# A ninth slot in the ring of expert weights, with its tables moved and turns of 36 parts

## The chip, the cores and the metric

The kernel runs on one core of one Trainium2 chip. The metric is the device time of one execution in microseconds (us). The core has TensorE (matmul), VectorE, ScalarE, GpSimd and SyncE. SyncE does no arithmetic here; it issues nearly all transfers, in the order in which they stand in its program.

## What is computed

One decoder layer for 256 prompt tokens and 8 sampled sequences of 4 tokens: a combined projection, retention and block-sparse attention, an output projection, and then a layer of 32 experts of which each token takes 4. All in float32. The change touches the expert layer alone:

```python
def moe(h, router_w, router_b, w_gu, b_gu, w_d, b_d):
    tok = h.reshape(-1, D_MODEL)
    logits = tok @ router_w + router_b
    top_v, top_i = lax.top_k(logits, TOP_K)
    top_w = jax.nn.softmax(top_v, axis=-1)
    gates = jnp.einsum('tk,tke->te', top_w, one_hot(top_i, N_EXPERTS))
    def expert(acc, xs):
        wgu, bgu, wd, bd, g = xs
        u = tok @ wgu + bgu
        glu = jnp.minimum(u[:, ::2], 7.0)
        lin = jnp.clip(u[:, 1::2], -7.0, 7.0)
        a = glu * jax.nn.sigmoid(1.702 * glu) * (lin + 1.0)
        return acc + g[:, None] * (a @ wd + bd), None
```

An expert has 8 MB of gate and up weights (1024 x 2048) and 4 MB of down weights (1024 x 1024), 384 MB for the 32.

## The kernel before

All of SBUF is one array, `arena`, of 53176 words on each of 128 partitions, and every tile is a fixed place in it (`at(start, dims)`). The program is written by hand for each engine, with semaphores between them.

**The stages.** Until about 310 us the projections, the two kinds of attention and the output projection run. Then comes the router, up to 325 us: TensorE multiplies by the router weights, VectorE takes the best four experts of each of three token tiles (`picked` marks them), and TensorE counts with three triangular or full matrices of ones (`earlier`, `ones`) which rank a token has at its expert (`count`, line 831). From the ranks VectorE makes selection matrices (`one_hot`, 1672), with which TensorE gathers up to 64 tokens of each expert of a pair (`gather`, 844).

**The expert loop.** 32 experts are 16 pairs. TensorE's `pair` (926) does the gate products of the first expert of a pair (four parts), its down products (two parts), the same for the second, and between them the transposes, the scatter of the pair before (`combine`) and the gather of the pair to come. `last_pair` (977) does pair 15 in another order. Lines 1063 to 1067 run pairs 0 to 13 in a loop of two pairs a pass and pairs 14 and 15 behind it. VectorE and ScalarE have loops of one pair.

**The ring.** An expert's weights come in `PARTS` = 6 parts of 2 MB, four of gate and up weights and two of down weights, 192 in all. Part n goes to slot n % 8. The eight slots of 4096 words lie in the first 32768 words of the arena, in space of the earlier stages, so that each opens when its stage is through (`PLACE`). SyncE issues parts 0 to 7 one by one behind such waits (lines 2019 to 2044); part 0 goes out at 263 us, parts 6 and 7 once the output projection is done, at 310. After that part n+8 waits until TensorE has used part n (`w_used`), in a loop of `TURN` = 24 parts a pass (2046 to 2051) and in straight code for the last 16 parts. The last one is fetched in two halves. TensorE waits for each part on the semaphore of its slot (`wt_in`).

**The tables.** `late` is one transfer of 304 KB (line 2030) with a count `iota`, the two counting matrices and an `expert` matrix of 32 columns. It stands at the end of the region Q (3328 words), which also holds the router's scratch: logits, `hot`, `picked`, `gates` sums and the scratch for pairs that need more rounds. Region MX (2304 words) follows Q. The scratch of further rounds is only used where an expert has more than 64 tokens; in these runs that branch isn't entered.

**Before the first pair.** Behind the gather of pair 0 TensorE counts the tokens of all experts (`count(3, ...)`, 1043), transposes the gates (1048), does two products that only keep it busy (`stay_awake`) and starts pair 0 once ScalarE has copied the gathered tokens and VectorE has made `esel` (1746). On VectorE the totals of the pairs (1734 to 1741), the quarter copies (1790) and the copy of the transposed gates (1794) stand ahead of that `esel`.

Of the kernel before, what the change touches and what calls it, by code (L numbers as in the profile page):

```python
# [23 lines left out]
I32 = mybir.dt.int32  # L24
# [21 lines left out]
RING = 8  # L46
# [122 lines left out]
def build_kernel(nc, t, table, outs):  # L169

    with ExitStack() as ctx:
# [20 lines left out]
        gate_slot = [at(WSLOT * place, 2, F2) for place in PLACE]  # L192
        down_slot = [at(WSLOT * place, 4, D) for place in PLACE]
# [25 lines left out]
        gain_in = at(cur, P); cur += P  # L219
        stat = at(cur, 64); cur += 64  # L220
        own_s = at(cur, 2, NS); cur += 2 * NS
# [39 lines left out]
        assert cur <= WORDS, cur  # L261

# [25 lines left out]
        sel = at(MX, TILES, 2, SLOTS)  # L288
        selg = at(MX + 384, TILES, 2, SLOTS)
        sgt = at(MX + 768, TILES * P)  # L290
        esel = at(MX + 1152, 2, SLOTS)
        rankm = at(MX + 1280, TILES, E + 2)
        gates = at(MX + 1280 + TILES * (E + 2), TILES, E + 2)
# [15 lines left out]
        pair_n = at(Q + 1032, PAIRS)  # L309
        flag = at(Q + 1048, 4, PAIRS)  # L310
        n_over_f = at(Q + 1112, 1)
        n_over_i = at(Q + 1113, 1).bitcast(I32)
        before = at(Q + 1114, 2, 64)
        work = at(Q + 1242, EXTRA, 64)
        work_f = at(Q + 2394, 2, EXTRA)
        work_i = at(Q + 2430, 2, EXTRA).bitcast(I32)
        pair_of = at(Q + 2466, 64)
        round_of = at(Q + 2530, 64)
        picked_off = at(Q + 2594, TILES, E)
        late = at(Q + 3328 - late_cols, late_cols)  # L320
        assert Q + 3328 - late_cols >= Q + 2690

        def late_const(name):
            a, n = table[name]
            return late[:, a - ncols:a - ncols + n]

        iota, earlier, ones = late_const("iota"), late_const("earlier"), late_const("ones")
# [88 lines left out]
        def _(pe):  # L416
# [409 lines left out]
            pe.wait_ge(late_in, 16)  # L826
# [14 lines left out]
            count(2, ones, 1, start=False, stop=True).then_inc(rank_full, 1)  # L841

# [1115 lines left out]
        def _(sp):  # L1958
# [51 lines left out]
            def load_turn(t):  # L2010
                load_part(t // PARTS, t % PARTS, t % RING)
# [99 lines left out]
```

## Time and profile before

| | |
|---|---|
| median of 3 runs | 1268.71 us (1266.96 to 1270.87) |
| the profiled execution | 1270.82 us |
| its span, first to last instruction | 1269.0 us |
| TensorE busy (matmuls) | 1207.8 us, 95% |
| VectorE, ScalarE, GpSimd busy | 384.2, 232.7, 120.3 us |
| moved | 500.64 MB, mean 395 GB/s |
| mean granted TensorE clock | 0.983 |

The span is cut on the page into 40 slices of 31.7 us:

```profile
PE   6999998699999999999999999999999999999997
PEclk8999999889899999999999999999999999999999
DMA  8999889968799999999999999999999999999994
GB/s 334 378 363 357 314 297 326 387 243 319 280 415 430 428 429 429 428 429 429 429 427 429 429 428 429 429 429 427 429 429 428 430 428 429 428 428 428 427 428 199
```

Each digit is the busy share of a slice in tenths, the last row what was moved. Both TensorE and the 16 DMA engines look full from the twelfth slice on. Matmuls are pipelined and their ends are modelled, so a busy TensorE isn't proof that it works at its peak, and which of the two bounds the loop has to be read from the chain of work that ended last and from the times between issue and landing of the transfers.

### The profile page before, as it was taken

Reading aid. Unit: us, or ns where it says so; the run is one execution under the profiler, and the core shown is the slowest. Engines: PE = TensorE matmul, PEld = TensorE weight load, DVE = VectorE, ACT = ScalarE, POOL = GpSimd, SP = SyncE. Lnnn points to the kernel's source line nnn. Section 1 sums busy time; section 2 is a strip of 40 time slices with the busy share of each in tenths; the row PEclk is TensorE's granted clock in tenths of the full one; section 3 lists DMA queues with packets and bytes.
Section 4 is the critical chain, followed back from the end, with each engine's and each line's share of the span. In section 5 each row is a group of like instructions: output and inputs, shape, how many; then the busy total and the mean of one; then the engine's idle time right before and its main releaser. Section 6 shows DMA issues by size and latency. Waiting matters only on the chain.

```text
span 1269.0 us, 17410 instructions
## 1 busy us (share of the span) xinstructions
PE 1207.8 (95%) x7256; PEld 517.4 (41%) x7256; DVE 384.2 (30%) x552; ACT 232.7 (18%) x529; POOL 120.3 (9%) x117
## 2 busy tenths in 40 slices
PE   6999998699999999999999999999999999999997
PEld 3455445345534434343433434343434434343432
DVE  4999964153411211111122111111112211111113
ACT  3021153024201121110112112010102121111103
POOL 2222446641000000000000000000000000000000
PEclk8999999889899999999999999999999999999999
DMA  8999889968799999999999999999999999999994
GB/s 334 378 363 357 314 297 326 387 243 319 280 415 430 428 429 429 428 429 429 429 427 429 429 428 429 429 429 427 429 429 428 430 428 429 428 428 428 427 428 199
DMA packets 56604, 500.64 MB, mean 395 GB/s; under 512 B 6393, under 2 KB 6801, under 8 KB 27761
## 3 DMA queue, kind: packets, MB, share of 16 engines
q1 hardware_dynamic: 42128, 430.55, 81.1%
q0 software_dynamic: 14432, 69.47, 14.7%
q8 instruction: 32, 0.52, 0.2%
q14 instruction: 12, 0.09, 0.0%
HBM read 495.29 MB, written 4.72 MB: 394 GB/s over the span
## 4 chain that ended last, share of the span: by engine, by line
PE 61%; DMA 26%; DVE 7%; issue 4%; ACT 1%; SPq 0%; POOL 0%; DVEq 0%; POOLq 0%; ACTq 0%
PE psum L940 22%; DMA arena<-w_gate_up 21%; PE psum L971 12%; PE psum L852 6%; DVE arena L1430 5%; DMA arena<-w_down 3%; PE psum L858 2%; PE psum L502 2%; PE psum L697 2%; PE psum L870 2%; PE psum L589 2%; PE psum L882 2%; DMA arena<-cache_k,arena 1%; PE psum L889 1%; PE psum L428 1%
## 5 line engine op out<-in xcount | busy, mean ns | idle before, releaser
L940 PE MATMUL psum<-arena 128*64 128x512 f32 x1920 | 422.7, 594 | 15.7 <-DMA arena<-w_gate_up 15.6
L940 PEld LDWEIGHTS psum<-arena 128*64 128x64 f32 x1920 | 134.8, 137 | 300.1 <-issue 265.0
L1758 DVE TENSOR_SCALAR arena<-psum 128x512 f32<-128x512 f32 x32 | 22.1, 692 | 682.8 <-PE psum L940 643.5
L971 PE MATMUL psum<-arena 128*64 128x512 f32 x960 | 212.6, 595 | 0.0
L1096 ACT ACTIVATE arena<-psum 64x512 f32<-64x512 f32 (+3 forms) x184 | 93.5, 509 | 370.2 <-PE psum L971 170.7
L1430 DVE STREAM_TRANSPOSE arena<-arena 128x2048 f32<-128x2048 f32 x32 | 121.4, 3920 | 3.1 <-PE psum L488 1.9
L971 PEld LDWEIGHTS psum<-arena 128*64 128x64 f32 x960 | 66.4, 137 | 124.2 <-issue 122.4
L502 PE MATMUL psum<-arena 128*128 128x512 f32 x224 | 107.1, 617 | 0.5 <-ACT arena L1096 0.4
L1313 ACT ACTIVATE arena<-arena 128x512 f32<-128x512 f32 x30 | 18.9, 631 | 419.4 <-DVE arena L1758 419.4
L1096 ACT ACTIVATE arena<-psum,arena 128x128 f32<-128x128 f32 (+2 forms) x182 | 53.6, 397 | 171.2 <-PE psum L502 115.8
L852 PE MATMUL psum<-arena 128*128 128x128 f32 x512 | 80.1, 302 | 0.4 <-DVE arena L1679 0.4
L852 PEld LDWEIGHTS psum<-arena 128*128 128x128 f32 x512 | 69.3, 206 | 17.7 <-issue 14.0
L1904 POOL DMA_INDIRECT arena<-cache_v,arena x64 | 70.4, 1100 | 50.9 <-PE psum L589 24.2
L870 PE MATMUL psum<-arena 128*128 128x512 f32 x128 | 63.5, 617 | 0.0
L502 PEld LDWEIGHTS psum<-arena 128*128 128x128 f32 x224 | 40.3, 192 | 46.6 <-issue 46.6
L1781 DVE TENSOR_TENSOR arena<-psum,arena 128x512 f32<-128x512 f32 (+1 forms) x80 | 48.0, 633 | 12.6 <-PE psum L870 12.6
L589 PE MATMUL psum<-arena 128*32 128x512 f32 x256 | 33.1, 653 | 13.5 <-DMA arena<-cache_v,arena 9.0
L488 PE MATMUL psum<-arena 128*32 128x128 f32 x1024 | 35.4, 280 | 7.6 <-DVE arena L1451 4.7
L1890 POOL DMA_INDIRECT arena<-cache_k,arena x32 | 32.3, 1010 | 100.3 <-DVE arena L1430 91.0
L488 PEld LDWEIGHTS psum<-arena 128*32 128x32 f32 x1024 | 26.7, 111 | 32.4 <-DVE arena L1430 17.0
L882 PE MATMUL psum<-arena 32*64 32x512 f32 x248 | 33.7, 613 | 1.0 <-DVE arena L1746 1.0
L870 PEld LDWEIGHTS psum<-arena 128*128 128x128 f32 x128 | 21.6, 188 | 28.8 <-issue 23.6
(242 smaller groups left out, 724.3 us busy)
## 6 DMA issues: line engine op xcount, KB each, us to landing
arena<-w_gate_up SPq DMA_DIRECT2D x128, 2048.0 KB, 29.7
arena<-w_down SPq DMA_DIRECT2D x63, 2048.0 KB, 32.9
arena<-w_in SPq DMA_DIRECT2D x7, 2048.0 KB, 18.3
arena<-w_out SPq DMA_DIRECT2D x2, 2048.0 KB, 13.9
out<-arena SPq DMA_DIRECT2D x4, 512.0 KB, 3.0
out<-arena POOLq DMA_DIRECT2D x1, 2048.0 KB, 12.5
arena<-w_down SPq DMA_DIRECT2D x2, 1024.0 KB, 34.0
arena<-x_prompt SPq DMA_DIRECT2D x2, 512.0 KB, 5.6
```

What stands on the lines that cost most here:

```text
L488: last = mm(psum[NS * c:NS * (c + 1), bank, P * (n % 4):P * (n % 4 + 1)], qk[:, g, 4 * c + x, :], kt[:, 4 * c + x, :], start=x == 0, stop= ...
L502: last = mm(psum[:, bank, :], h_t[:, k, tile * P:(tile + 1) * P], w[:, k, :], start=k == 0, stop=k == KC - 1)
L589: last = mm(psum[NS * s:NS * (s + 1), 6 + g, :], pt_sb[:, v % 2, j * P + s:(j + 1) * P:4], v_raw(n)[:, s, 512 * r:512 * (r + 1)], start=False,
L852: mm(o, hn[:, tile, cols], sel[:, tile].rearrange("p a b -> p (a b)"), start=tile == 0, stop=False, skip_group_check=True)
L870: last = mm(psum[:, 3 + half, :], sgt[:, P * tile:P * (tile + 1)], out2[:, 512 * half:512 * (half + 1)], start=True, stop=True)
L882: mm(psum[64 * g:64 * (g + 1), b, :], esel[E * b:E * (b + 1), e, :], bgu[E * b:E * (b + 1), g, :], start=True, stop=False, skip_group_chec ...
L940: last = mm(psum[64 * g:64 * (g + 1), b, :], xt[:, 2 * kk + m, lhs], gate_slot[slot][:, m, c:c + 512], start=False, stop=kk == 3 and m == ...
L971: last = mm(psum[64 * g:64 * (g + 1), 2, :], at_sb[:, m, SLOTS * q:SLOTS * (q + 1)], down_slot[slot][:, m, 512 * g:512 * (g + 1)], start=q ...
L1096: return nc.scalar.activation(out, in_, ACT.Copy, scale=scale)
L1430: v.transpose(kt_sb[:, u % 2, :].rearrange("p (e b r) -> p r e b", e=16, b=32), k_raw[:, u % 4, :]).then_inc(k_trans, 1)
L1781: v.tensor_tensor(dst, got, dst, ALU.add).then_inc(comb_added, 1)
L1904: pool.indirect_dma_start(out=v_raw(n)[:, s, :], out_offset=None, in_=cv, in_offset=bass.IndirectOffsetOnAxis(ap=row, axis=0), bounds_chec ...
```

## The change

- `RING` is 9. The ninth slot is words Q to Q + 4095: all of region Q and the first 768 words of MX. The order of the parts stays; part n goes to slot n % 9.
- What lived there moves: the tables `iota` and `earlier` to words of the softmax scratch of the attention (`LT`), `ones` to the place of `gain_in`, the selection matrices, `rankm` and `gates` 768 words up in MX, the scratch of further rounds to the cosine table's place behind the router weights and to other dead places.
- The tables come in three transfers in place of one. They are issued before `x_sample` and wait for the second normalisation of the attention (`o_norm` 2), where before they were issued behind part 2.
- Part 8 is issued behind part 7, after waits for both counts of the router (`rank_full` 2) and for `gates_ready`.
- The count over all experts moves from behind the gather to ahead of it, and to PSUM bank 0.
- TensorE's loop has three pairs a pass and five passes, with pair 15 behind it; SyncE's has 36 parts a pass and four passes, with 39 parts of straight code behind it.

```diff
-RING = 8
+RING = 9
...
-        gate_slot = [at(WSLOT * place, 2, F2) for place in PLACE]
-        down_slot = [at(WSLOT * place, 4, D) for place in PLACE]
...
+        SLOT_AT = [WSLOT * place for place in PLACE] + [Q]
+        assert len(SLOT_AT) == RING and MX == Q + 3328
+        gate_slot = [at(a, 2, F2) for a in SLOT_AT]
+        down_slot = [at(a, 4, D) for a in SLOT_AT]
...
-        late = at(Q + 3328 - late_cols, late_cols)
...
+        late_at = {"iota": LT, "earlier": LT + 320, "expert": LT + 448}
...
             count(2, ones, 1, start=False, stop=True).then_inc(rank_full, 1)
+            for tile in range(TILES):
+                last = mm(psum[:, 0, 0:E], ones, picked[:, tile, :], start=tile == 0, stop=tile == TILES - 1)
+            last.then_inc(rank_full, 1)
...
             gather(0, 1)
-            for tile in range(TILES):
-                last = count(3, ones, tile, start=tile == 0, stop=tile == TILES - 1)
-            last.then_inc(rank_full, 1)
             pe.wait_ge(gates_ready, 1)
...
-                return lambda part: ((12 * half + part) % RING, i * 48 + 16 * ((12 * half + part) // RING + 1))
+                return lambda part: ((12 * half + part) % RING, i * 64 + 16 * ((12 * half + part) // RING + 1))
...
-            with pe.Fori(0, PAIRS // 2 - 1) as i:
-                pair(i * 2, in_turn(i, 0), True)
-                pair(i * 2 + 1, in_turn(i, 1), True)
-            pair(PAIRS - 2, in_turn(PAIRS // 2 - 1, 0), True)
-            last_pair(PAIRS - 1, in_turn(PAIRS // 2 - 1, 1))
+            with pe.Fori(0, PAIRS // 3) as i:
+                for third in range(3):
+                    pair(i * 3 + third, in_turn(i, third), True)
+            last_pair(PAIRS - 1, in_turn(PAIRS // 3, 0))
...
             sp.wait_ge(*mark["pt7"])
+            sp.wait_ge(o_norm, 2)
+            a = table["iota"][0]
+            sp.dma_start(at(LT, 448), t["shape_consts"][:, a:a + 448]).then_inc(late_in, 16)
+            for dst, name in ((ones, "ones"), (late_const("expert"), "expert")):
+                a, n = table[name]
+                sp.dma_start(dst, t["shape_consts"][:, a:a + n]).then_inc(late_in, 16)
             sp.wait_ge(y_zero, 1)
...
-            sp.dma_start(late, t["shape_consts"][:, ncols:ncols + late_cols]).then_inc(late_in, 16)
...
             load_turn(7)
-
-            TURN = 24
-            with sp.Fori(0, (E * PARTS - RING) // TURN) as i:
+            sp.wait_ge(rank_full, 2)
+            sp.wait_ge(gates_ready, 1)
+            load_turn(8)
+
+            TURN, TURNS = 36, 4
+            with sp.Fori(0, TURNS) as i:
                 for u in range(TURN):
                     part = RING + u
                     sp.wait_ge(w_used, i * TURN + (u + 1))
-                    load_part(i * 4 + part // PARTS, part % PARTS, part % RING)
-            for part in range(RING + (E * PARTS - RING) // TURN * TURN, E * PARTS):
+                    load_part(i * 6 + part // PARTS, part % PARTS, part % RING)
+            for part in range(RING + TURNS * TURN, E * PARTS):
```

## Rows read from the trace of the kernel before

**Rows 1.** The chain that ended last, from 341 us: start, duration, what.

```profile
341.52 13.88 PE psum L940 x64
...
397.53 13.88 PE psum L940 x64
...
740.74 30.58 DMA arena<-w_gate_up
...
1065.01 3.65 PE psum L940 x16
...
1123.74 3.65 PE psum L940 x16
...
1183.62 3.65 PE psum L940 x16
...
1202.16 7.04 PE psum L991 x32
...
1242.36 3.65 PE psum L1007 x16
```

**Rows 2.** Windows: length, busy us (records) by engine, clock, DMA share, GB/s.

```profile
400.00:500.00 100.00, 100.00 (x505) 39.95 (x502) 19.41 (x33) 12.91 (x25) 0.00 (x0) 1.00 1.01 428
...
335.00:340.00 5.00, 4.45 (x24) 2.88 (x22) 2.33 (x10) 3.32 (x9) 0.00 (x0) 0.91 0.89 374
340.00:345.00 5.00, 4.57 (x26) 1.48 (x28) 1.68 (x5) 0.14 (x1) 0.00 (x0) 1.00 0.04 18
345.00:350.00 5.00, 5.00 (x26) 1.66 (x24) 0.00 (x0) 0.00 (x0) 0.00 (x0) 1.00 0.77 252
```

**Rows 3.** Transfers of line 2008 in 800 to 1200 us.

```profile
DMA to landing us min/median/max: 29.7/33.0/36.4
```

**Rows 4.** Timeline of VectorE and ScalarE before pair 0: start, duration, instruction.

```profile
327.92 0.26 DVE L1732 TENSOR_TENSOR arena<-arena 128x96 f32<-128x96 f32 x1
...
339.51 0.55 DVE L1794 COPY arena<-psum 32x384 f32<-32x384 f32 x1
...
336.66 2.17 ACT L1096 ACTIVATE arena<-psum,arena 128x128 f32<-128x128 f32 x8 [12.26 <-PE psum L858]
```

**Rows 5.** Timeline of TensorE around the gather, and one gather in the loop.

```profile
324.60 1.10 PE L443 MATMUL psum<-arena 128*128 128x512 f32 x2
326.11 2.05 PE L852 MATMUL psum<-arena 128*128 128x128 f32 x8 [0.40 <-DVE arena L1679]
...
336.55 0.85 PE L831 MATMUL psum<-arena 128*128 128x32 f32 x6
...
340.43 1.09 PE L882 MATMUL psum<-arena 32*64 32x512 f32 x8 [0.98 <-DVE arena L1746]
...
382.57 1.23 PE L852 MATMUL psum<-arena 128*128 128x128 f32 x8
```

**Rows 6.** Windows of one microsecond where the clock changes.

```profile
325.00:326.00 1.00, 0.71 (x2) 0.00 (x0) 0.93 (x4) 0.00 (x0) 0.00 (x0) 0.81 1.05 442
...
335.00:336.00 1.00, 1.00 (x7) 0.99 (x5) 0.00 (x0) 0.00 (x0) 0.00 (x0) 0.57 1.18 492
```

**Rows 7.** Timeline of SyncE's issues, and the second normalisation on VectorE.

```profile
225.10 2.35 SPq L2015 DMA_DIRECT2D arena<-router_b  x1
...
291.29 0.33 SPq L2023 DMA_DIRECT2D arena<-x_sample  x1
...
295.82 1.38 SPq L2030 DMA_DIRECT2D arena<-shape_consts  x1
...
287.47 0.75 DVE L1482 TENSOR_SCALAR arena<-psum,arena 128x512 f32<-128x512 f32 x1
```

**Rows 8.** Packets, MB and share by queue, in 340:450, 450:1100 and 1100:1215 us.

```profile
q8 instruction: 4, 0.07, 0.2%
...
q1 hardware_dynamic: 19128, 278.54, 100.7%
...
q8 instruction: 3, 0.05, 0.2%
```

More of the change, by code:

```diff
@@ L218, in build_kernel @@
         gain = at(cur, 28); cur += 28
-        gain_in = at(cur, P); cur += P
+        gain_in = at(cur, P)
+        ones = at(cur, P); cur += P
         stat = at(cur, 64); cur += 64
+        LT = cur
         own_s = at(cur, 2, NS); cur += 2 * NS
@@ L287, in build_kernel @@
         at_last = at(HT, 4, P)
[L288 to L293, printed above, removed]
+        sel = at(MX + 768, TILES, 2, SLOTS)
+        selg = at(MX + 1152, TILES, 2, SLOTS)
+        sgt = at(MX + 1536, TILES * P)
+        esel = at(MX + 1920, 2, SLOTS)
+        rankm = at(MX + 2048, TILES, E + 2)
+        gates = at(MX + 2048 + TILES * (E + 2), TILES, E + 2)
+        assert 2048 + 2 * TILES * (E + 2) <= 2304
         squares = at(HT, D)
@@ L308, in build_kernel @@
         picked = at(Q + 936, TILES, E)
[L309 to L318, printed above, removed]
+        RW = C0 + table["cos"][0]
+        pair_n = at(RW, PAIRS)
+        flag = at(RW + 16, 4, PAIRS)
+        n_over_f = at(RW + 80, 1)
+        n_over_i = at(RW + 81, 1).bitcast(I32)
+        work_f = at(RW + 82, 2, EXTRA)
+        work_i = at(RW + 118, 2, EXTRA).bitcast(I32)
+        before = at(RW + 154, 2, 64)
+        assert 282 <= (KC + 1) * E
+        pair_of = at(Z + 4352, 64)
+        round_of = at(Z + 4416, 64)
+        work = at(HT, EXTRA, 64)
         picked_off = at(Q + 2594, TILES, E)
-        late = at(Q + 3328 - late_cols, late_cols)
-        assert Q + 3328 - late_cols >= Q + 2690
+        late_at = {"iota": LT, "earlier": LT + 320, "expert": LT + 448}
+        assert LT + 480 <= HT and table["earlier"][0] == table["iota"][0] + 320
         def late_const(name):
-            a, n = table[name]
-            return late[:, a - ncols:a - ncols + n]
-        iota, earlier, ones = late_const("iota"), late_const("earlier"), late_const("ones")
+            return at(late_at[name], table[name][1])
+        iota, earlier = late_const("iota"), late_const("earlier")
         rw = at(C0 + table["cos"][0], KC, E)
@@ L825, in _ @@
             logits(1).then_inc(lg_full, 1)
-            pe.wait_ge(late_in, 16)
+            pe.wait_ge(late_in, 48)
             def count(tile, lhs, src, **flags):
@@ L1054, in in_turn @@
             def in_turn(i, half):
-                return lambda part: ((12 * half + part) % RING, i * 48 + 16 * ((12 * half + part) // RING + 1))
+                return lambda part: ((12 * half + part) % RING, i * 64 + 16 * ((12 * half + part) // RING + 1))
             def in_extra(n):
-                return lambda part: (part % RING, n * 32 + (16 * (part // RING) - 112)) if part % RING < 4 else \
-                    (part, n * 16 + 144)
-            with pe.Fori(0, PAIRS // 2 - 1) as i:
-                pair(i * 2, in_turn(i, 0), True)
-                pair(i * 2 + 1, in_turn(i, 1), True)
-            pair(PAIRS - 2, in_turn(PAIRS // 2 - 1, 0), True)
-            last_pair(PAIRS - 1, in_turn(PAIRS // 2 - 1, 1))
+                return lambda part: (part % RING, n * 32 + (16 * (part // RING) - 144)) if part % RING < 3 else \
+                    (part, n * 16 + 96)
+            with pe.Fori(0, PAIRS // 3) as i:
+                for third in range(3):
+                    pair(i * 3 + third, in_turn(i, third), True)
+            last_pair(PAIRS - 1, in_turn(PAIRS // 3, 0))
             more = extra_pairs(pe)
@@ L1688, in _ @@
             dve.wait_ge(router_in, 32)
-            dve.wait_ge(late_in, 16)
+            dve.wait_ge(late_in, 48)
             for tile in (0, 2, 1):
```

6 lines of the change are left out of this document (3 added, 3 removed).

## The prediction

> **What bounds the kernel now.** I read the chain that ended last first, because two engines look full on the page. In it [rows 1] TensorE sets the pace at first: the first gate product of pair 0 starts at 341.52 us, that of pair 1 at 397.53, so a pair takes 56.01. At 740.74 a transfer of expert weights enters the chain, and from there the same point of each pair comes every 58.73 us (1065.01 to 1123.74). Twelve parts of 2 MB in 58.73 us are 4.89 us a part, 429 GB/s, and the windows show that rate from 400 us on already [rows 2]. So the transfers never rest in the expert loop, also while TensorE seems to lead: they are the bound, and TensorE only works off the lead of eight parts that it starts with, 58.73 - 56.01 = 2.72 us a pair. Issue to landing says the same: 33 us, nearly seven parts in flight [rows 3].
>
> A stream that never rests is only shortened by an earlier start or fewer bytes. The windows show where it rested [rows 2]: 374 GB/s in 335 to 340, 18 in 340 to 345, 252 in 345 to 350. Against 429 that loses 5 x (0.13 + 0.96 + 0.41) = 7.5 us. There all eight slots are full and TensorE has not yet emptied the first (a part takes it 13.88 / 4 = 3.5 us from 341.5 on). The slack of TensorE against the stream: at 56.01 a pair, pair 15 would start at 341.52 + 15 x 56.01 = 1181.7; it starts at 1202.16 [rows 1]. That is 20.5 us.
>
> **Part by part.**
> *Ninth slot.* Part 8 is issued once gates are ready, at 328.2 [rows 4], behind parts 6 and 7, which keep the queue busy until about 340 [rows 2]. It so fills 4.89 of the 7.5 us of rest; the 11 us between issue and need are its cover. From then on part n+9 waits for the use of part n, as part n+8 did: the stream keeps the same rhythm against TensorE with one part less to go, **-4.89**. What is queued behind the new waits on SyncE is only the loop, which waits for TensorE's first part anyway.
>
> *All pairs counted ahead of the gather.* Six records (0.85 us, 336.55) move to before the stay-awake product at 324.60 [rows 5]. That product then ends at about 326.5 to 327.2 instead of 325.7, and the gather, which began at 326.11, starts 0.4 to 1.1 us later. The clock fell to the 1.2 GHz level at 325.6 (mean 0.81 in that microsecond) and was back at 2.4 late in the microsecond from 335 (0.57) [rows 6]; work pushed past the rise runs twice as fast, so the gather ends only 0.2 to 0.6 later. ScalarE took 2.17 us from 336.66 to copy it, to 338.83 [rows 4]; that becomes 339.0 to 339.4. VectorE's side was later: its totals, flags, quarter copies and the copy of 339.51 (0.55) led to TensorE's start at 340.43, with 0.98 idle [rows 4, 5]. The totals and copies now run during the gather, where VectorE was idle for 9 us, and the transposes that feed the copy follow the gather at once. Late next are ScalarE's copy and the second stay-awake product (twice the 1.10 us of the one at 324.60 less its overlap, from about 337.4), both near 339.4. TensorE starts 0.9 us earlier (bounds 0 and 1.2), hence also the restart of the stream: **-0.9**. It leaves 7.5 - 4.9 - 0.9 = 1.7 us of rest.
>
> *Tables moved.* Instead of one issue of 1.38 us at 295.82, SyncE makes three once the second normalisation is through (287.47 + 0.75), ahead of the issue at 291.29 [rows 7]. Three such are 4.1 us, ending at 292.4: x_sample and parts 1 and 2 go out about 1.2 us later, from part 3 on SyncE is level again, and 304 KB leave the busy queue. The slowest issue of 128 short rows near by took 2.35 us [rows 7]; three of them make part 1 4 us and part 3 some 2.6 us later. The first case costs nothing and the last 1 us, beyond the 1.7 us of rest. I take **0**.
>
> *Loop bodies of three pairs.* TensorE's loop grows from two pairs to three, SyncE's from 24 parts to 36. Fetches of instructions show as queue 8. In 340 to 450, the first pass, it moved 4 packets of 16 KB; from 450 to 1100 none; after the loop it moves again [rows 8]. So two pairs stay resident. 505 + 502 records in 100 us [rows 2] are 564 in a pair's 56; the 1,108 records of 110 us took 4 packets, 277 a packet. The body held was thus four packets and its ends, six or seven. Three pairs are 1,692 records: 6.1 packets, eight with the ends, nine with the one fetched ahead. No row shows nine held. If they are not, each of the four returns fetches up to nine again, 36 packets. Their price: three packets in 115 us at 0.2% of 16 engines are 1.2 us of one engine each [rows 8]. The first one after the loop made a pair 59.88 us, 1.15 more; the next twelve parts took 58.74 again (1183.62 to 1242.36) though further packets fell there [rows 1, 8], so they go to different engines. 36 x 1.15 to 1.5 / 16 = 2.6 to 3.4; I take **+3.0**. The ends are 0 (held) and 36 x 1.15 / 3 = 13.8 (each three cost as the three after the loop did). I choose the refetch because the new body is half as long again as the longest that a row shows held. The tail and the moved scratch words change no count of instructions: 0.
>
> The Trainium skill, page "Runtime: NRT & Kernel Launch", section "Instruction fetch mechanics", speaks against this change: TensorE's instruction memory is a FIFO of 128 KiB, 2048 instructions, in blocks of 16 KiB, and a taken branch to a block outside the window forces a fetch. By that rule nine blocks don't fit into eight and the time is 1265.9; were the body held, 1262.9. The trace agrees on the 16 KB and shows at least six blocks held; its sentence on a window of two pages is not borne out.
>
> **Sum.** -4.89 - 0.9 + 0 + 3.0 = -2.8. The profiled execution had a span of 1269.0 and a time of 1270.8: 1266.2 and 1268.0. Against the median of the runs, 1268.7, it is **1265.9**.
>
> **Rivals.**
> 1. *The longer body is held*, or only the block at its seam is fetched again (2 packets a return, 8 in all, 0.6 us). For it: nothing shows a limit. Then -5.8 or -5.2: 1262.9 to 1263.5.
> 2. *The gap is smaller than in this profile.* With the gather at 2.4 GHz (8 records in 1.23 us, not 2.05 [rows 5]) TensorE starts up to 4.4 us earlier, the stream rests less, and part 8 ends after TensorE's first part. The runs spread over 4 us, and the profiled one is among the slowest, which speaks for it. The gain then falls by up to 2 us, the same as with the late issues above; with refetches 1267 to 1268.
> 3. *Slower: each return of TensorE's loop stands still until the block has come.* Four stalls of X delay pair 15 to 1181.7 - 0.9 + 4X; the slack of 20.5 us hides them until X = 5.3. With X = 8 TensorE becomes the bound and pair 15 starts at 1212.8, 10.6 us late: 1279.3. Slower by over 0.3% from X = 6.3. For it: transfers wait 33 us in the loaded queues [rows 3]; against it: packets of queue 8 hold an engine only 1.2 us, and no stall shows in the first pass. Fetches at 13.8 us would give 1276.7, on the same side.
> 4. *Nothing gained though part 8 is early*, if the start of TensorE slips (1.2 GHz in the first two parts: the first takes 3.5 us longer, the second outlasts a transfer by 2.1): 1269.4 to 1271.5.
>
> **Chances.** Forecast 0.45 (own range 1264.5 to 1267.5), rival 1 0.27, rival 2 0.13, rival 3 0.10, rival 4 0.05. A measurement tells about 0.3%, 3.8 us, from no change: faster means under 1264.9. Rival 1 and a fifth of the forecast and little else lie there, together 0.38; 0.52 within; 0.10 slower. The range runs from 1261.5 (rival 1 with the whole rest of 7.5 us gone) to 1270, leaving out rival 3 and part of 4.
>
> **What would show it.** The windows at 340 to 350 near 429 GB/s but for 1.7 us; a SyncE issue near 328; landing in the settled loop at 38 us rather than 33; TensorE's first gate product at 340.6; starvation of TensorE beginning some two pairs later (5 us at 2.72 a pair). The queue-8 row decides between forecast and rival 1: near 68 packets or 32; the settled pair 58.7 to 59. Wrong would be the forecast if the stream's rate fell for another reason, or if TensorE's pairs showed gaps at every third.

## The result and the profile after

| | before | changed |
|---|---|---|
| median, min to max (5 runs each) | 1266.96 us (1265.82 to 1270.87) | 1259.31 us (1258.33 to 1260.89) |
| ratio, 95% interval | | 0.9934 [0.9915, 0.9952] |
| profiled execution, its span | 1270.82, 1269.0 us | 1259.37, 1257.6 us |
| mean granted clock of it | 0.983 | 0.986 |

The changed kernel is 7.65 us faster in these runs by the medians. The forecast was 1265.9, in a range of 1261.5 to 1270, so the time lies below the range. The same kernel was timed twice more, in two jobs of the experiments (e_after_again and e_after_third), on chips where all kernels take about 30 us longer ahead of the router: 4.9 and 6.6 us by the medians, with ratios of 0.9971 [0.9956, 0.9987] and 0.9955 [0.9939, 0.9971]. The comparisons are of fast runs; the one slow run, 4778.74 us in e_warm_before, is left out.

First the row on which forecast and first rival part. This is the page's list of queues for the changed kernel, and under it the queue's rows for the windows 340 to 450, 450 to 1100 and 1100 to 1215 us (queue: packets, MB, share), as in [rows 8].

```profile
q8 instruction: 32, 0.52, 0.2%
...
q8 instruction: 4, 0.07, 0.2%
...
q8 instruction: 2, 0.03, 0.0%
...
q8 instruction: 1, 0.02, 0.1%
```

32 packets, as many as in before, not 68. The two between 450 and 1100 are at 454.7 and 481.3 us, still in the first pass, which ends at 505; at the four returns of the loop nothing is fetched. The body of three pairs is held.

The windows around the start of pair 0 (columns as in [rows 2]):

```profile
330.00:335.00 5.00, 5.00 (x36) 3.79 (x35) 0.31 (x1) 1.15 (x5) 0.00 (x0) 1.00 1.02 429
335.00:340.00 5.00, 4.79 (x25) 1.40 (x25) 1.87 (x5) 2.31 (x5) 0.00 (x0) 1.00 0.98 415
340.00:345.00 5.00, 5.00 (x26) 1.62 (x24) 0.00 (x0) 0.00 (x0) 0.00 (x0) 1.00 0.96 364
345.00:350.00 5.00, 5.00 (x26) 1.68 (x24) 0.00 (x0) 0.00 (x0) 0.00 (x0) 1.00 1.00 426
400.00:500.00 100.00, 100.00 (x510) 40.72 (x508) 19.96 (x34) 15.11 (x33) 0.00 (x0) 1.00 1.01 427
```

Against 429 GB/s the three from 335 to 350 lose 5 x (0.03 + 0.15 + 0.01) = 1.0 us, where [rows 2] lost 7.5. The stream hardly rests any more. SyncE's timeline shows why (start, duration, line, how many):

```profile
309.18 32.23 SPq L2012 DMA_DIRECT2D arena<-w_gate_up  x4
```

The group of four is parts 6 to 9. Its third, part 8, is out at 327.8 (the end of the group when the timeline is cut at 330 us); its last, part 9, goes out at 341, once TensorE has used part 0.

TensorE ahead of pair 0 (timeline), which answers to [rows 5]:

```profile
323.79 1.47 PE L848 MATMUL psum<-arena 128*128 128x32 f32 x6
325.07 2.05 PE L448 MATMUL psum<-arena 128*128 128x512 f32 x2
326.92 1.67 PE L860 MATMUL psum<-arena 128*128 128x128 f32 x8
...
334.07 1.88 PE L448 MATMUL psum<-arena 128*128 128x512 f32 x4
336.16 1.09 PE L890 MATMUL psum<-arena 32*64 32x512 f32 x8 [0.21 <-ACT arena L1100]
337.18 4.08 PE L948 MATMUL psum<-arena 128*64 128x512 f32 x18
```

The six counting records are now ahead of the gather (323.79). What comes last before pair 0 (its bias products, here line 890) is ScalarE's copy, with 0.21 us of idle time, where VectorE's `esel` cost 0.98. The first gate product is at 337.2 instead of 341.5, 4.3 us earlier. Only 0.7 of that is the change's (measured in e_count_ahead below); 2.5 is the clock, which in the profile of before was low for 10.2 us in the gather [rows 6] and here for 6.9 (321.3 to 328.2, from the granted clock of one-microsecond windows), and 1.1 comes from the stages ahead of the router, which the change doesn't touch.

The chain that ended last (start, duration, what):

```profile
337.25 13.88 PE psum L948 x64
...
393.26 13.88 PE psum L948 x64
...
845.15 34.66 DMA arena<-w_gate_up
...
960.89 36.38 DMA arena<-w_gate_up
...
1136.94 36.52 DMA arena<-w_gate_up
...
1195.67 36.50 DMA arena<-w_down
1232.16 0.04 issue
1232.21 3.65 PE psum L1015 x16
```

A pair takes 56.01 us at first (337.25 to 393.26), and transfers enter at 845.15 rather than at 740.74 [rows 1], nearly two pairs later, as forecast. Three pairs from 960.89 to 1136.94 are 58.68 each: the settled pace is untouched. From issue to landing a gate transfer now takes longer, in the settled loop:

```profile
DMA to landing us min/median/max: 31.2/37.7/40.3
```

37.7 against 33.0 [rows 3], which at 4.89 us a part is nearly eight parts in flight where there were nearly seven.

### The profile page after: what moved, and what is told of

It is laid out like the page before. It is cut to its first block, busy times and chain, and to the rows that moved or that the text cites. A ratio compares the mean times of both kernels' runs of the same rounds, so it can differ in the third digit from the quotient of the medians.

```text
span 1257.6 us, 17335 instructions
## 1 busy us (share of the span) xinstructions
PE 1203.2 (96%) x7256; PEld 515.9 (41%) x7256; DVE 384.2 (31%) x552; ACT 233.1 (19%) x529; POOL 120.1 (10%) x117
## 4 chain that ended last, share of the span: by engine, by line
PE 64%; DMA 23%; DVE 7%; issue 4%; ACT 2%; SPq 0%; POOL 0%; POOLq 0%; DVEq 0%; ACTq 0%
PE psum L948 23%; DMA arena<-w_gate_up 17%; PE psum L979 13%; PE psum L860 6%; DVE arena L1434 5%; DMA arena<-w_down 3%; PE psum L878 3%; PE psum L702 2%; PE psum L866 2%; PE psum L594 2%; PE psum L890 2%; PE psum L507 2%; DMA arena<-cache_k,arena 2%; PE psum L897 1%; PE psum L433 1%
## 5 line engine op out<-in xcount | busy, mean ns | idle before, releaser
L860 PE MATMUL psum<-arena 128*128 128x128 f32 x512 | 77.3, 294 | 0.0
L493 PEld LDWEIGHTS psum<-arena 128*32 128x32 f32 x1024 | 26.7, 111 | 32.3 <-DVE arena L1434 17.1
```

Source lines behind the costliest of these rows:

```text
L493: last = mm(psum[NS * c:NS * (c + 1), bank, P * (n % 4):P * (n % 4 + 1)], qk[:, g, 4 * c + x, :], kt[:, 4 * c + x, :], start=x == 0, stop= ...
L860: mm(o, hn[:, tile, cols], sel[:, tile].rearrange("p a b -> p (a b)"), start=tile == 0, stop=False, skip_group_check=True)
```

## The experiments

Three measures are used. **The ratio** on record, with its 95% interval, for each kernel against before in the same job, which runs on one chip. It can differ from the ratio of the medians (0.9971 against 0.9963 in e_after_again). **At equal clock**: each timed run lists the mean granted clock of TensorE. Within a job a least-squares line through all runs, with an offset for each kernel, has a slope of -1.0 to -1.1 us for +0.001 of clock and leaves 1.2 to 1.6 us of scatter; the offset is the difference to before with the clock's luck taken out, given with its 95% interval. Where an edit is meant to act on the clock, this measure takes out the very effect that is looked for. **The stream**: in the one profile of each kernel, the time from the first gate product of pair 0 to the end of the last transfer in the chain, so for before 1209.22 + 33.09 - 341.45 (where TensorE's timeline has that product) = 900.9 us. It holds nothing of the stages ahead.

| kernel (its job) | ratio, 95% | equal clock, us | stream, us | end of stream to end of span, us |
|---|---|---|---|---|
| before | | | 900.9 | 26.7 |
| changed | 0.9934 [0.9915, 0.9952] | | 895.0 | 25.4 |
| e_count_ahead (1) | 0.9983 [0.9968, 0.9998] | -1.0 ± 1.0 | 900.0 | 26.9 |
| e_count_behind (1) | 0.9968 [0.9952, 0.9985] | -4.7 ± 1.0 | 895.5 | 25.0 |
| e_tables_late (1) | 0.9967 [0.9951, 0.9983] | -4.6 ± 1.0 | 896.6 | 25.1 |
| e_part8_late (1) | 0.9992 [0.9977, 1.0007] | -2.2 ± 1.0 | 898.6 | 26.7 |
| e_four_pairs (2) | 1.0038 [1.0016, 1.0059] | +3.2 ± 0.9 | 906.5 | 25.0 |
| e_warm_before (2) | 1.0007 [0.9987, 1.0026] | +0.6 ± 0.9 | 900.9 | 26.7 |
| e_warm_after (2) | 0.9956 [0.9937, 0.9974] | -4.3 ± 0.9 | 896.2 | 25.1 |
| e_early (2) | 0.9956 [0.9937, 0.9975] | -5.9 ± 0.9 | 895.5 | 25.5 |
| e_after_again (3) | 0.9971 [0.9956, 0.9987] | -5.75 ± 0.8 | 895.3 | 26.9 |
| e_slot_only (3) | 0.9974 [0.9956, 0.9991] | -4.35 ± 0.8 | 895.1 | 25.1 |
| e_delay_before (3) | 1.0011 [0.9994, 1.0028] | +1.9 ± 0.8 | 900.3 | 27.2 |
| e_delay_after (3) | 0.9980 [0.9965, 0.9995] | -2.9 ± 0.8 | 895.6 | 25.5 |
| e_after_third (4) | 0.9955 [0.9939, 0.9971] | -5.75 ± 1.4 | 896.1 | 25.0 |
| e_early_warm (4) | 0.9916 [0.9885, 0.9948] | -5.3 ± 1.7 | 896.2 | 25.4 |
| e_straight (4) | 0.9996 [0.9979, 1.0014] | +1.6 ± 1.2 | 901.7 | 25.2 |
| e_four_again (4) | 1.0045 [1.0028, 1.0062] | +3.2 ± 1.4 | 906.4 | 25.1 |

Stream column: the four kernels with eight slots and the loop of before (before, e_count_ahead, e_warm_before, e_delay_before) lie from 900.0 to 900.9, mean 900.5; the ten with nine slots and part 8 early from 895.0 to 896.6, mean 895.7. **That is 4.8 us apart, and a part of the stream is 4.89.**

### Is it the slot: one part of the change at a time

**e_slot_only** is the changed kernel with the count behind the gather and the tables behind part 2 again, so that only the slot and the turns are left:

```diff
             count(2, ones, 1, start=False, stop=True).then_inc(rank_full, 1)
-            for tile in range(TILES):
-                last = mm(psum[:, 0, 0:E], ones, picked[:, tile, :], start=tile == 0, stop=tile == TILES - 1)
-            last.then_inc(rank_full, 1)
...
             gather(0, 1)
+            for tile in range(TILES):
+                last = mm(psum[:, 0, 0:E], ones, picked[:, tile, :], start=tile == 0, stop=tile == TILES - 1)
+            last.then_inc(rank_full, 1)
...
-            sp.wait_ge(o_norm, 2)
-            a = table["iota"][0]
-            sp.dma_start(at(LT, 448), t["shape_consts"][:, a:a + 448]).then_inc(late_in, 16)
...
             sp.wait_ge(st2_ready, 1)
+            sp.wait_ge(o_norm, 2)
+            a = table["iota"][0]
+            sp.dma_start(at(LT, 448), t["shape_consts"][:, a:a + 448]).then_inc(late_in, 16)
...
```

> The changed kernel with both helpers undone: the count stands behind the gather again, and the tables go out behind part 2. What is left is the ninth slot with its longer turns. Theory A: each helper is worth 0.5 to 2 us once the stream no longer rests, so 1.5 to 3 us slower than the changed kernel and 3 to 5 faster than before. Theory E, only the ninth slot counts: as the changed kernel.

Measured: -4.35 us at equal clock, and 895.1 in the stream, the same as with everything. Against e_after_again in the same job (-5.75) the other edits together are worth 1.4 ± 0.9 us.

**e_after_again** and **e_after_third** are the changed kernel unaltered, in jobs 3 and 4.

> The changed kernel once more, as a control on the chip of the three that follow: 0.9934 of the time before, as first measured, or up to 0.996 if that chip was kind to it. Theory A needs it to lie at least 4 us under the variant in which part 8 waits (0.9992).

> The changed kernel once more, unaltered. If the ninth slot with the count ahead is worth what the comparisons at equal clock gave so far (5.75 us), the ratio is 0.9955 within 0.0010. If the first measurement was the true size (7.65 us), it is 0.994. If most of it was luck of the clock, it is over 0.998.

Measured: -5.75 twice at equal clock, with medians of 1291.23 and 1290.64 us. That is the sum of the forecast without its refetch, -5.8.

**e_part8_late** keeps nine slots, but part 8 waits until TensorE has used part 0, as the ninth part of before did:

```diff
             sp.wait_ge(gates_ready, 1)
+            sp.wait_ge(w_used, 1)
             load_turn(8)
```

> The changed kernel in which part 8 waits until TensorE has used part 0, so the ninth slot stays empty during the first rest of the stream and all else is as changed. Theory A: the rest is back and one part (4.9 us) is lost, less what the early start of TensorE leaves of it: 1263.5 to 1265. Theory E, the gain comes from the deeper ring or the longer passes: 1259.3.

Measured: 0.9992, at equal clock -2.2, and the rest of the stream is back. Its windows, with the first gate product at 344.2 us in this profile:

```profile
340.00:345.00 5.00, 4.80 (x27) 1.95 (x27) 2.17 (x5) 3.45 (x9) 0.00 (x0) 1.00 0.89 374
345.00:350.00 5.00, 5.00 (x26) 1.72 (x24) 0.00 (x0) 0.00 (x0) 0.00 (x0) 1.00 0.34 77
350.00:355.00 5.00, 5.00 (x26) 1.61 (x24) 0.00 (x0) 0.00 (x0) 0.00 (x0) 1.00 0.96 400
355.00:360.00 5.00, 5.00 (x22) 1.52 (x18) 1.77 (x3) 0.63 (x1) 0.00 (x0) 1.00 1.01 433
...
365.00:370.00 5.00, 5.00 (x26) 1.73 (x24) 0.00 (x0) 0.15 (x1) 0.00 (x0) 1.00 1.01 429
```

So most of the gain is that part 8 moves in the gap, not that there is room for nine. The slot alone still takes 1.9 us off the stream (898.6 against 900.5), and 1.5 ± 1.0 off the time, once the 0.7 us of the count ahead are taken from the 2.2. One part of it can be seen: before has a second, small gap 24 us after the start of pair 0 (357 GB/s in 365 to 370 of its windows, 0.8 us lost), when TensorE gathers and frees nothing; here two parts go out together at 347.9 and it is gone. The other 1.1 us is within what one profile differs from the next.

### The helpers: count ahead, and the place of the tables

**e_count_ahead** is before with that edit alone, **e_count_behind** the changed kernel with it taken back:

```diff
             count(2, ones, 1, start=False, stop=True).then_inc(rank_full, 1)
+            for tile in range(TILES):
+                last = mm(psum[:, 0, 0:E], ones, picked[:, tile, :], start=tile == 0, stop=tile == TILES - 1)
+            last.then_inc(rank_full, 1)
...
-            tot = psum[:, 5, 3 * E:4 * E].rearrange("p (n e) -> p n e", e=2)
+            tot = psum[:, 0, 0:E].rearrange("p (n e) -> p n e", e=2)
```

> The kernel before with the count over all pairs moved ahead of the gather and nothing else (eight slots, two pairs a pass). Theory A, the stream of weights is the bound and with eight slots it restarts when TensorE frees its first part: TensorE starts 0.9 to 3 us earlier and the whole of it is gained, 1264 to 1266 against 1267 us. Theory B, all of the change's gain is the ninth slot: 1267, no difference, whatever TensorE's start does.

> The changed kernel with the count put back behind the gather (part 8 then goes out some 8 us later, at about 337 us, still before the queue is dry at about 340). Theory A with nine slots: the stream ends part 8 at 343 to 344, and TensorE's first part used decides only if it is later than about 342; a start 0.9 us later costs 0 to 1.5 us: 1259.5 to 1261. Theory C, the early start of TensorE carries the gain that was not forecast (3 to 4 us): 1262 to 1263.

Measured: -1.0 ± 1.0 at equal clock in before. In the profiles with the same two stretches at the low clock level, from the first router product to the first gate product it takes 24.3 to 24.5 us with the count ahead and 25.0 to 25.1 with it behind, so **0.7 us**. The idle time before the bias product is what is saved. This is its row in e_slot_only, where the count is behind; it answers to the 0.21 us of the changed kernel above.

```profile
369.04 1.09 PE L887 MATMUL psum<-arena 32*64 32x512 f32 x8 [0.99 <-DVE arena L1750]
```

**e_tables_late** is the changed kernel with the three transfers of the tables behind part 2, where before has its one.

> The changed kernel with the three transfers of the tables issued where the one transfer stood before, behind part 2. Theory A: the stream no longer rests at 340, so 304 KB put back ahead of part 3 delay all that follows by 0.7 to 1.3 us: 1260 to 1260.7 against 1259.3. Theory D, a rest is left in the stream that absorbs it: 1259.3.

Measured: 0.9967 and -4.6 ± 1.0, next to -4.7 for e_count_behind in the same job. The changed kernel itself was not in that job; against its -5.75 in two others the early place of the tables is worth 1.1 ± 1.3 us. A cost of moving them to the front is excluded as far as this resolution goes, a gain isn't shown.

### Does the start of TensorE count, now that the stream rests less

With nine slots the gap of the stream is nearly full, and a rival to "every microsecond of TensorE's start counts" was that part 8 now hides it. **e_delay_before** and **e_delay_after** give both kernels eight more keep-awake products ahead of pair 0:

```diff
-            stay_awake(4, 2)
+            stay_awake(4, 6)
             pe.wait_ge(bias_in, 48)
```

> The kernel before with four more products that only keep TensorE busy ahead of pair 0 (3.8 us at 2.4 GHz), so TensorE starts pair 0 some 3 to 3.8 us later. Theory A, with eight slots the stream restarts when TensorE has used part 0: slower by the whole 3 to 3.8 us, 1.0025 to 1.003. Theory B, TensorE's start doesn't matter because it has slack of 20 us later: no difference.

> The changed kernel with the same four products. Theory A: part 8 ends at about 343.5 and part 9 goes out at about 341 us, so some 2 us of the delay are hidden: slower than the changed kernel by 1.5 to 2.5 us. Theory B: no difference; theory C, the start counts in full with nine slots too: 3 to 3.8 us.

Measured: +1.9 ± 0.8 and, against e_after_again, -2.9 + 5.75 = +2.8 ± 0.9. The stream is 900.3 and 895.6, unchanged. In e_delay_after these products last until the bias product starts, where the changed kernel waits for ScalarE's copy:

```profile
366.10 5.32 PE L448 MATMUL psum<-arena 128*128 128x512 f32 x12
371.35 1.09 PE L890 MATMUL psum<-arena 32*64 32x512 f32 x8
```

That is 5.32 - 1.88 = 3.4 us more of them, less the waits that they cover (0.98 and 0.21 us), so 2.4 and 3.2 us. The times alone, with their intervals, would also allow that some 1 us is hidden. The stream decides: had part 8 hidden 1 to 2 us of the delay, it would be that much shorter than 895.7, and it is 895.6. The windows show the same. Behind the first gate product at 372.4 us the transfers now rest, for 5 x (0.12 + 0.51) = 3.1 us:

```profile
370.00:375.00 5.00, 5.00 (x25) 1.48 (x25) 0.00 (x0) 0.00 (x0) 0.00 (x0) 1.00 0.90 378
375.00:380.00 5.00, 5.00 (x26) 1.72 (x24) 0.00 (x0) 0.00 (x0) 0.00 (x0) 1.00 0.68 210
```

So a later start costs its full length with either ring: the ninth slot doesn't hide it, because part 9 still waits for the use of part 0.

**e_early** issues part 1 one stage earlier, ahead of the tables, and the last gain vector behind part 4.

```diff
             sp.wait_ge(*mark["pt7"])
+            sp.wait_ge(v_used, V_SETS - 1)
+            load_turn(1)
             sp.wait_ge(o_norm, 2)
...
-            sp.dma_start(f_gain, t["final_norm_g"].partition_broadcast(P)).then_inc(fg_in, 16)
-            sp.wait_ge(v_used, V_SETS - 1)
-            load_turn(1)
...
             load_turn(4)
+            sp.dma_start(f_gain, t["final_norm_g"].partition_broadcast(P)).then_inc(fg_in, 16)
```

> The changed kernel with part 1 issued as soon as its slot is free (about 286 us) in place of behind the tables and x_sample, and the gains of the last norm issued behind part 4. The queue rested from 285 to 290 us. Theory A: the stream starts up to 5 us earlier, but with nine slots full it rests again until TensorE has used its first part at about 341, so only the 1 to 2 us are gained by which part 8 ended later than that: 1257.5 to 1258.5. Theory H, an earlier start is gained in full: 1254 to 1255.

Measured: -5.9 ± 0.9, beside e_warm_after's -4.3 in the same job and the changed kernel's -5.75 in others. All nine slots are now full early, and the gap is open again: 93 GB/s in the window 367 to 372, around the first gate product at 366.9.

```profile
362.00:367.00 5.00, 4.80 (x29) 2.42 (x31) 2.17 (x5) 3.38 (x9) 0.00 (x0) 1.00 1.04 436
367.00:372.00 5.00, 5.00 (x25) 1.71 (x26) 0.00 (x0) 0.08 (x1) 0.00 (x0) 1.00 0.27 93
```

The stream takes 895.5 us all the same. What counts is how many parts have come when TensorE starts; weights that come sooner than that give nothing here. Whether a tenth slot would use them was not tested.

### The clock

**e_warm_before** and **e_warm_after** put four products that only keep TensorE busy ahead of the router's products and two behind them, where it waits for VectorE.

```diff
+            stay_awake(4, 2)
             pe.wait_ge(a_empty, n_0[0])
...
             logits(1).then_inc(lg_full, 1)
+            stay_awake(7, 1)
```

> The kernel before with three more products that only keep TensorE busy, two while it waits for the copies of the normalised tokens (312 us) and one while it waits for the first choice of experts (322 us). Theory A: if the clock stays at 2.4 GHz in the gather, TensorE starts pair 0 up to 4 us earlier, and with eight slots all of it is gained, 1263 to 1265. Theory B: 1267. If the clock falls all the same, 1267 too, and the clock row tells.

> The changed kernel with the same three products. Theory A: with nine slots the stream itself, which ends part 8 at 343 to 344, is late next, so an earlier start of TensorE is worth under 1 us: 1258.5 to 1259.3. Theory C, TensorE's start still sets the end: 1256 to 1257.

Measured: +0.6 ± 0.9 and -4.3 ± 0.9 at equal clock, but this edit is meant to act on the clock, so the plain times count here: -0.65 us by the medians in before (1296.68 against 1297.33) and -6.25 in the changed kernel, which in two other jobs had -4.9 and -6.6. Neither is shown to be better than without. The first of the two falls around the router is gone, and the second is still there (351 to 358 us in e_warm_after): from router to pair 0 it took 23.9 us rather than 24.4, half a microsecond, which the runs can't tell apart.

**e_early_warm** joins e_early and e_warm_after.

> The changed kernel with part 1 of the expert weights issued one layer-stage wait earlier and with TensorE kept busy by idle matmuls ahead of the router. If the two edits act on different things (a transfer and the clock) and both are worth what they were alone at equal clock (part 1 early about 1.5 us more than the changed kernel by one comparison and 0.1 by the other; the idle matmuls nothing), it is at most 1.5 us below the changed kernel of this job. If both are noise it equals it within 1 us. If the idle matmuls stand in the way, it is 1 us or more above it.

Measured: median 1289.67 us beside 1290.64 for e_after_third, -5.3 ± 1.7 at equal clock, stream 896.2. That its ratio is as low as 0.9916 comes from two of six runs (1278.73 and 1281.57 us) with a clock of 0.985 and 0.983. Nothing is seen to add up; no version beats the changed kernel by more than the runs tell apart.

### The limit on the loop body

**e_four_pairs** is before, eight slots, with a body of four pairs, three passes, and four pairs behind it. **e_four_again** is the same beside e_straight.

```diff
-            with pe.Fori(0, PAIRS // 2 - 1) as i:
-                pair(i * 2, in_turn(i, 0), True)
-                pair(i * 2 + 1, in_turn(i, 1), True)
-            pair(PAIRS - 2, in_turn(PAIRS // 2 - 1, 0), True)
-            last_pair(PAIRS - 1, in_turn(PAIRS // 2 - 1, 1))
+            with pe.Fori(0, PAIRS // 4 - 1) as i:
+                for quarter in range(4):
+                    pair(i * 4 + quarter, in_turn(i, quarter), True)
+            for quarter in range(3):
+                pair(PAIRS - 4 + quarter, in_turn(PAIRS // 4 - 1, quarter), True)
+            last_pair(PAIRS - 1, in_turn(PAIRS // 4 - 1, 3))
```

> The kernel before with TensorE's loop four pairs a pass (three passes, four pairs of straight code behind) and eight slots. The forecast's step: a body that is longer than what stays resident is fetched again at each return. Theory F, the limit lies between three and four pairs (three pairs showed no refetch in the changed kernel): two returns fetch 9 to 11 packets each, 50 or more packets of queue 8 in place of 32, and the time rises by 1.5 to 3 us. Theory G, what was fetched once stays, however long the body: 32 packets or a few more for the longer straight code, 1267 us.

> The kernel with the body of four pairs once more, beside the one with straight code. If its loss is refetch at the returns, it is again 3 to 5 us above the kernel before (1.0025 to 1.004), with some 60 packets of q8, and 3 us above the kernel with straight code. If its loss was the chip's, it is within 1 us of the kernel before.

Measured: 1.0038 and 1.0045, 5.1 and 5.2 us by the medians, where the expectation was 1.5 to 3, and 906.5 and 906.4 in the stream, 5.9 more than the mean of eight slots. At equal clock it is 3.2 both times, which is too little: the falls of the clock at the returns (below) are this kernel's own and shouldn't be taken out. The page of e_four_again, and its queue 8 in 450 to 1100 us:

```profile
q8 instruction: 63, 1.03, 0.3%
...
q8 instruction: 29, 0.48, 0.3%
```

Before has none in that stretch [rows 8]. The packets come one every 20 to 30 us through the whole second pass as well, 11 of them: the whole body is fetched again, each block as TensorE gets near it. And at each return TensorE stands still. Its timeline there:

```profile
587.81 3.17 PE L971 MATMUL psum<-arena 128*64 128x512 f32 x14
593.64 1.42 PE L882 MATMUL psum<-arena 32*64 32x512 f32 x8 [2.65 <-issue]
594.99 11.41 PE L940 MATMUL psum<-arena 128*64 128x512 f32 x46
```

2.65 us in which TensorE waits for nothing that the profile shows, and 2.40 at the second return, 5.1 us together. That it waits for instructions is inferred from the packets around it; no other kernel here stands so at a return. The clock then falls for 3.4 us (0.93 in the window 590 to 595 and 0.73 in 595 to 600), so the products behind it take longer too.

**e_straight** has the same amount of TensorE code as e_four_again, eight pairs written out, but a body of two: five passes, then pairs 10 to 14 and the last.

```diff
-            with pe.Fori(0, PAIRS // 2 - 1) as i:
+            with pe.Fori(0, PAIRS // 2 - 3) as i:
...
-            pair(PAIRS - 2, in_turn(PAIRS // 2 - 1, 0), True)
+            for n in range(PAIRS - 6, PAIRS - 1):
+                pair(n, in_turn(n // 2, n % 2), True)
```

> The kernel before with the loop of two pairs passed five times instead of seven, and four more pairs written out behind it: TensorE then has as much code as with the body of four pairs (eight pairs in all), but its body is still that of two. If the loss with four pairs is refetch of the body at its returns, this kernel has about 9 packets of q8 more than the kernel before (32 to about 41), none of them spread over the passes of the loop but all in the stretch of the straight pairs, and its time is that of the kernel before within 1 us. If straight code costs as much as refetched code, it is 2 to 4 us slower, as the kernel with four pairs is.

Measured: 0.9996 [0.9979, 1.0014], +1.6 ± 1.2 at equal clock. 41 packets, 9 more than before, and in the passes behind the first none; they come again from about 940 us on, behind the loop. The stream is 901.7, 1.2 more than the mean of eight slots, against 906.4 for e_four_again. So longer code costs 0 to 2 us, and 4.7 us of the four-pair kernel's 5.9 in the stream come with its 22 further packets and two returns. Where do they go? The chain of e_four_again steps from transfer to transfer, once these lead:

```profile
944.60 34.22 DMA arena<-w_gate_up
...
1004.60 33.23 DMA arena<-w_gate_up
...
1063.61 32.95 DMA arena<-w_gate_up
...
1122.34 34.24 DMA arena<-w_gate_up
...
1182.23 33.38 DMA arena<-w_gate_up
```

The steps are 60.00, 59.01, 58.73 and 59.89 where the settled one is 58.73. The two that are 1.2 to 1.3 us longer are the size of the one step that before has behind its loop [rows 1]. In e_straight too the steps are 58.7 as long as no packet comes; behind its loop, from 940 us on, the first packets leave the step as it is, and then one step is 60.20:

```profile
1002.45 32.92 DMA arena<-w_gate_up
1061.15 34.42 DMA arena<-w_gate_up
1121.35 32.99 DMA arena<-w_gate_up
```

A packet costs 5.9 / 31 = 0.19 us on average in e_four_again, and 1.2 / 9 = 0.13 in e_straight; the second rests on 1.2 us, not much more than the 0.9 by which streams of eight slots differ. Whether the stand at the return adds to that could not be told apart: the chain gives it no share, since TensorE is ahead of the stream's need at both returns (transfers enter only at 887.74), and the stream loses only 0.3 us around the first (423 GB/s in 585 to 610) and 0.2 around the second (426 in 815 to 840).

## Why the prediction was wrong, and where it was right

**The failed step is the last one, the loop bodies of three pairs.** It put +3.0 for a refetch of nine blocks at each of four returns, because no row showed nine held. There was none; this term is 0, and rival 1 was the case. The three-pair body is held and the four-pair body isn't: the limit lies between 1,692 and some 2,260 records of TensorE. The count was of the right kind: the body of four was in fact fetched again as a whole at every return. What was wrong was to turn "no row shows it held" into "likely refetched". The rows bore out neither, so chances of 0.45 and 0.27 in that order had no row behind them. The count hung on one block. e_straight needs 9 packets for four more pairs, 2.25 a pair, so a body of three is 6.8 blocks and one of four 9.0; by the 11 packets of a second pass they are 8.2 and 11. The forecast had counted 6.1 for three pairs and then added two ends and one fetched ahead, which made nine; the body of two pairs, which it took for six or seven blocks held, is 4.5 by the same 2.25. The Trainium skill, page "Runtime: NRT & Kernel Launch", section "Instruction fetch mechanics", has 128 KiB, 2048 instructions, in TensorE's memory, refilled in blocks of 16 KiB, which makes eight. The runs don't contradict that: the body held is near or under eight blocks, the one that isn't is over it. The same section's stall of a taken branch to a page that isn't there agrees with the 2.65 us of e_four_again.

**The price of a refetch** was too low as well: 36 packets at 3.0 us are 0.083 each, and the runs show 0.13 to 0.19, about twice that. By it a refetch would have cost 5 to 7 us, not 3.0, inside the bounds of 0 and 13.8. It didn't matter, since nothing was fetched.

**The ninth slot, -4.89**: 4.8 in the stream (900.5 to 895.7), and -4.35 ± 0.8 at equal clock with only the slot. Right. The argument from the gap held too: with part 8 outside the gap more than half of it is gone (e_part8_late), and the settled pace is the same 58.7 us a pair. What the forecast didn't have is the 1.9 us that a ninth slot takes off the stream even when part 8 comes after the gap.

**All pairs counted ahead, -0.9** (0 to 1.2): 0.7 measured. Right, and as put there, ScalarE's copy is late next, with 0.21 us. That TensorE's start counts in full, which this term took for granted, was shown by the two delays.

**Tables moved, 0** (0 to 1): no cost is seen, but the runs resolve only about 1 us. Three issues took 0.34 + 0.91 = 1.25 us, and not 4.1, and x_sample went out at 290.12 instead of 291.29, with all stages 1.1 us earlier in that profile.

**The sum** without the failed term is -5.8; two measurements at equal clock gave -5.75. From the median of 1268.7 that is 1262.9, inside the range, and the first measurement gave 1259.3, below it. So the failed term is 3.0 of the 6.6 us by which the forecast missed; the other 3.6 came from the base and the clock, which the forecast took as fixed. The median of before itself was 1266.96 in that comparison, 1.75 below the one given, and 7.65 - 5.8 = 1.9 us remain. The clocks on record account for them. The five runs of the changed kernel list 0.986 to 0.989, mean 0.9874; the 33 runs of before in job 1, on a chip with the same times (median 1267.72), have a mean of 0.9847. Put on the line of that job, the first measurement is -5.8 ± 1.4 us at equal clock. It joins runs of two jobs, for the clocks of before in the first comparison are on record for one run only (0.983), so it is strong evidence and not a proof.

One such piece of luck can be seen in the profiles, a fall of the clock behind the stream, in the last 27 us. A window of before:

```profile
1258.00:1259.00 1.00, 1.00 (x2) 0.34 (x1) 0.00 (x0) 1.00 (x1) 0.00 (x0) 0.50 0.00 0
```

Of the changed kernel, at the same work:

```profile
1248.00:1249.00 1.00, 1.00 (x5) 0.60 (x4) 0.00 (x0) 0.98 (x3) 0.00 (x0) 1.00 0.00 0
```

And of the changed kernel once more, in the profile of e_after_again:

```profile
1281.00:1282.00 1.00, 1.00 (x2) 0.34 (x1) 0.00 (x0) 1.00 (x1) 0.00 (x0) 0.50 0.00 0
```

TensorE idles in all three, 2.25, 2.66 and 2.55 us for the last sums, and then has a few products left. They run at 1.2, 2.4 and 1.2 GHz, and from the end of the stream to the end of the span it is 26.7, 25.4 and 26.9 us. The table's last column has about 25 or about 27 for every kernel. The same program, changed, has 25.4, 26.9 and 25.0 in its three profiles, so the fall belongs to the execution and not to the change, and its 1.5 us are luck.

**Rival 2**, the gap smaller than in the profile, was right in its first half. The profile of before had the low clock for 3.4 us at the router's products and then for 10.2 in the gather [rows 5, 6], where most of the others had 3.4 and 6.9, the second only partly in the gather: its first gate product comes 2.5 us later for that. In windows of 2 us from 10 us before the first gate product to 12 behind it, before loses 7.7 us of transfer, and e_count_ahead, e_warm_before, e_straight and e_four_again 5.4 to 7.2. But the gain did not shrink: e_early, in which all nine parts came well before TensorE's start, has the same stream (895.5) as the others.

**Rival 3**, a stand at each return, was real as a mechanism but in the four-pair kernels only, at 1.9 to 2.65 us rather than 8, where it said that up to 5.3 us would be hidden. **Rival 4** didn't occur.

**The range** ended at 1261.5, with about the whole gap of 7.5 us filled and nothing for the luck of the clock and the median of three runs. Medians of before alone were 1266.96, 1267.72 and 1268.71. That is 1.75 us, and a range that reaches to the best case has to have it on top.

## What to carry to other kernels

Where transfers bound a loop and never rest in it, look for the windows where they do rest, and count how many parts are there when the consumer starts: here a slot more was worth one part's time when it was filled by then, 1.9 us when it was filled after, and parts that came sooner gave nothing. Before counting a longer loop body as a loss, look at the instruction queue's packets per pass; here a body of 1,692 records of TensorE was held and one of some 2,260 was not, and writing out four pairs behind the loop cost 0 to 2 us. For differences of 0.3%, compare at equal clock or by a stretch that holds only the work in question, since the clock's falls move a run by more than that.

## What was not expected of the hardware

- A loop body of TensorE of three pairs is held whole, and one of four is fetched again whole: 63 packets of 16 KB on queue 8 instead of 32, 11 in the second pass, with 1.9 to 2.65 us of standing at a return.
- A fetched block costs the weight stream 0.13 to 0.19 us on average, though it holds one of 16 DMA engines for about 1.1 us (an estimate: 0.3% of 16 engines for 650 us, shared by 29 packets), which spread evenly would be 0.07. Part of it comes as single steps of 1.2 to 1.5 us between pairs, and some packets have no cost that shows.
- The fall of the clock behind an idle stretch of TensorE isn't the same in each execution of one program: in the changed kernel's profiles the clock was at 2.4 GHz after 2.66 us of idle time and at 1.2 after 2.55. The mean clock of a run, listed to 0.001, tells its time to 1.2 to 1.6 us.
